# HGRN2 layers: the value projection token-major for two heads, the values matmuls moved into the next head's scores visit

## The reference, cut to what matters

```
h = rms_norm(x, norm_w[layer])
q, f, inp_v, g = jnp.split(h @ w_in, 4, axis=-1)
q = silu(q); k = (1.0 - lb) * sigmoid(-f)
log_f = log(lb + (1 - lb) * sigmoid(f))          # forget gate, per channel
# with b the running sum of log_f over the tokens, and state 0 at the start:
o[t] = sum_{s<=t} (q[t] . k[s] . exp(b[t] - b[s])) v[s]
o = rms_norm(o, o_norm_w) per head
x = x + (o * silu(g)) @ w_out
```

## Time and profile before

| | us |
|---|---|
| median of 3 runs | 1348.59 (1348.59 to 1348.66) |
| span of the profiled execution | 1346.8 |
| TensorE matmul busy in it | 1339.1 (99%) |
| VectorE busy | 923.1 (69%) |
| ScalarE busy | 687.2 (51%) |
| GpSimd busy | 145.3 (11%) |
| granted TensorE clock | 1.00 |

### The profile page before, as it was taken

How to read it: one execution, slowest core, us unless ns; L and a number is a source line. 1 busy time by engine, 2 the same in 40 slices (tenths; PEclk the granted TensorE clock), 3 DMA queues, 4 the chain that set the end, 5 groups by cost and what they waited for, 6 DMA issues and landing times.

```text
span 1346.8 us, 22178 instructions
## 1 busy us (share of the span) xinstructions
PE 1339.1 (99%) x8759; PEld 1118.0 (83%) x8759; DVE 923.1 (69%) x1659; ACT 687.2 (51%) x1226; POOL 145.3 (11%) x224
## 2 busy tenths in 40 slices
PE   9999999999999999999999999999999999999999
PEld 8888888888888888888888887788888888888887
DVE  7867778564767576666676676865657577777782
ACT  6445555353655565656565656553434335454550
POOL 2422333000000000000000000000000022332220
DMA  6322233423222222222223131332333322232221
GB/s 194 95 80 79 64 94 95 118 79 91 66 79 79 79 79 79 79 79 79 79 68 90 48 92 50 105 93 71 94 94 94 110 76 83 63 93 76 84 64 63
DMA packets 211688, 113.62 MB, mean 84 GB/s; under 512 B 3743, under 2 KB 209889, under 8 KB 211586
## 3 DMA queue, kind: packets, MB, share of 16 engines
q1 hardware_dynamic: 211202, 112.02, 28.9%
q0 software_dynamic: 384, 0.20, 0.1%
HBM read 110.10 MB, written 2.10 MB: 83 GB/s over the span
## 4 chain that ended last, share of the span: by engine, by line
PE 96%; DVE 2%; ACT 1%; issue 1%; DMA 0%; SPq 0%; ACTq 0%; DVEq 0%
PE ps L647 39%; PE ps L662 38%; PE scores L662 4%; PE ps L1088 2%; PE ps L1072 2%; PE ps L1028 2%; PE ps L881 1%; PE scores L1056 1%; PE ps L1056 1%; PE scores L852 1%; PE ps L676 1%; PE ps L883 1%; PE scores L870 1%; PE scores L819 1%; PE ps L892 1%
## 5 line engine op out<-in xcount | busy, mean ns | idle before, releaser
L647 PE MATMUL ps<-op_hi,w_hi 128*128 128x512 f32 (+1 forms) x800 | 311.7, 390 | 0.0
L647 PE MATMUL ps<-op_lo,w_hi 128*128 128x512 f32 (+1 forms) x800 | 305.4, 382 | 0.0
L647 PE MATMUL ps<-op_hi,w_lo 128*128 128x512 f32 (+1 forms) x800 | 304.5, 381 | 0.0
L662 PE MATMUL ps<-w_hi,op_hi 128*128 128x512 f32 (+1 forms) x728 | 294.0, 404 | 1.6 <-DVE op_lo L1844 1.6
L662 PE MATMUL ps<-w_lo,op_hi 128*128 128x512 f32 (+1 forms) x728 | 282.6, 388 | 0.0
L662 PE MATMUL ps<-w_hi,op_lo 128*128 128x512 f32 (+1 forms) x728 | 282.2, 388 | 0.0
L1786 DVE TENSOR_TENSOR w_lo<-raw,w_hi 128x1024 fp32r<-128x1024 f32 x200 | 245.1, 1251 | 12.4 <-ACT w_hi L1274 10.9
L1274 ACT ACTIVATE w_hi<-raw 128x1024 fp32r<-128x1024 f32 x200 | 203.0, 1052 | 26.8 <-PE ps L662 11.2
L647 PEld LDWEIGHTS ps<-op_lo,w_hi 128*128 128x128 f32 x800 | 150.4, 188 | 29.9
L647 PEld LDWEIGHTS ps<-op_hi,w_hi 128*128 128x128 f32 x800 | 150.5, 188 | 27.4 <-DVE op_lo L1829 0.2
L647 PEld LDWEIGHTS ps<-op_hi,w_lo 128*128 128x128 f32 x800 | 150.7, 188 | 27.0
(11 more groups left out here) (228 smaller groups left out, 1944.9 us busy)
## 6 DMA issues: line engine op xcount, KB each, us to landing
raw<-in_b_w_in SPq DMA_DIRECT2D x80, 512.0 KB, 3.9
raw<-in_a_w_in SPq DMA_DIRECT2D x64, 512.0 KB, 4.2
raw<-in_c_w_in SPq DMA_DIRECT2D x24, 512.0 KB, 4.1
raw<-in_a_w_out SPq DMA_DIRECT2D x16, 512.0 KB, 4.3
raw<-in_b_w_out SPq DMA_DIRECT2D x8, 512.0 KB, 4.0
raw<-in_c_w_out SPq DMA_DIRECT2D x8, 512.0 KB, 4.9
xt<-in_x SPq DMA_DIRECT2D x4, 512.0 KB, 6.2
y<-in_norm_w SPq DMA_DIRECT2D x3, 512.0 KB, 4.7
```

Source lines behind the costliest of these rows:

```text
L647: last = nc.tensor.matmul(bank, a, b, start=(k == 0 and p == 0), stop=(k == KT - 1 and p == 2))
L662: last = nc.tensor.matmul(bank, a, b, start=(k == 0 and p == 0), stop=(k == KT - 1 and p == 2))
```

## The change

The diff does four things, all in the HGRN2 layers.

1. Step range 16-23 is now `v_step`: v is projected token-major, for a pair of heads at once, two of the four token tiles in each body. An even body i does token tiles 0 and 1 of heads i and i+1, an odd one tiles 2 and 3 of the same pair. A body does 48 matmuls 256 wide in place of 24 matmuls 512 wide. The v weights of head i+1 are loaded and split in body i (body 0 has five chunks, body 7 three); four ring slots hold the v weights, `a_v01` and `a_v23` the results.
2. `turn_v`, `v_out`, `a_v`, `a_vt` and their semaphores are gone.
3. `values(h-1)` stands ahead of `scores` in the visit after step 6 of the next body, `states` and `turn_o` go from the visit after step 20 to one after step 26. The squares, the root, `o_squares` and `o_norm` of a head move into the next body with it.
4. The last move of the queries (`last_move`) writes into a buffer of its own, `a_qf`; it is two VectorE instructions (a copy of one half, a multiply of the other) in place of one. `a_on` shares the buffer of `a_sq`.

```diff
-        a_v, at = carve(at, 2, S)
+        a_v01, at = carve(at, 4, 2 * P)
+        a_v23, at = carve(at, 2, 2 * P)
-        a_vt, at = carve(at, TT, P)
-        a_on, at = carve(at, TT, P)
+        a_on = a_sq
+        a_qf, at = carve(at, S)
...
+def a_order(i):
+    of_v = ((2, 0), (2, 1)) if i == 0 else ((2, i + 1),) if i + 1 < HEADS else ()
+    return ((1, i), (0, i)) + of_v + ((3, i),)
...
+        def v_half(of):
+            return a_v23 if of % 2 else a_v01[:, of // 2 % 2 * 2:of // 2 % 2 * 2 + 2]
+        def v_tile(head, t):
+            return v_half(head // 2 * 2 + t // 2)[:, t % 2, head % 2 * P:(head % 2 + 1) * P]
...
# TensorE
-                    def turn_v():
...
+                    def v_step(k):
+                        slot = a_v_slot(i // 2 * 2)
+                        for half in (2 * k, 2 * k + 1):
+                            t, of = divmod(half, KT)
+                            last = token_step(acc[0][:, t * 2 * P:(t + 1) * 2 * P], slice(slot, slot + 2), of,
+                                              i % 2 * 2 + t)
+                        return last
...
                     def states():
-                        pe.wait_ge(vT_done, h + 1)
+                        pe.wait_ge(v_act, h // 2 * 2 + 2)
...
                     if mix and not proj:
-                        turn_v()
                         gate_bank(3, 4, 5, 6, 7)
+                        values(h - 1)
                         scores()
...
-                        steps[17] = [turn_v, turn_k]
-                        steps[20] = [turn_o, states] if end else [states]
-                        steps[25] = [values]
-                        steps[6] = [scores]
+                        steps[17] = [turn_k]
+                        steps[26] = [turn_o, states] if end else [states]
+                        steps[6] = [lambda: values(h - 1), scores] if end else [scores]
...
# ScalarE
+                    def square(of):
+                        act.wait_ge(o_ready, of + 1)
...
-                        split_chunks(IN0[n], per, j, par, (2, 3), ring)
+                        for part, of in a_order(i)[2:]:
+                            split_part(i, part, of)
...
                         nc.scalar.activation(a_sig[:, 2], acc[0][:], ACT.Sigmoid, scale=-1.0).then_inc(f_act, 1)
+                        if end:
+                            square(h - 1)
...
                         if mix:
-                            v_out()
                             k_out()
+                        if end:
+                            root(h - 1)
...
# VectorE
-                        move_queries(6, a_q2[:, 0], h, prev, 4)
+                        last_move()
...
-                    split_lo_chunk(IN0[n], len(A_PARTS), j, par, 3, ring)
+                    split_part(i, 3, i)
+                    if end:
+                        o_squares(h - 1)
...
+                    if end:
+                        o_norm(h - 1)
+                    move_queries(0, a_q[:, par], head, par, 0)
+                    far_queries(0)
+                    farthest_queries(0)
+                    if not last_proj:
+                        for part in (1, 0):
+                            split_part(i + 1, part, i + 1)
+                    next_queries(0)
+                    far_queries(1)
+                    farthest_queries(1)
                     if mix:
                         carry()
                     if end:
                         into_y()
...
-                    if mix and not last_proj:
-                        o_squares(h)
-                    next_queries(0)
-                    if mix and not last_proj:
-                        o_norm(h)
...
+                    next_queries(1)
+                    far_queries(2)
+                    farthest_queries(2)
```

More of the change, by code:

```diff
@@ L86, with a_number, a_v_slot, a_ring @@
 ACC0 = [sum(ACC_OF[:n]) for n in range(4)]
[L89 to L96, removed]
+def a_order(i):
+    of_v = ((2, 0), (2, 1)) if i == 0 else ((2, i + 1),) if i + 1 < HEADS else ()
+    return ((1, i), (0, i)) + of_v + ((3, i),)
+def a_number(i, part, head):
+    return sum(len(a_order(n)) for n in range(i)) + a_order(i).index((part, head))
+def a_v_slot(head):
+    return (HALF + 2, HALF)[head // 2 % 2] + head % 2
+def a_ring(part, head):
+    return (1, 0, a_v_slot(head), SLOTS - 1 if head == HEADS - 1 else 2)[part]
 def b_ring(par, c):
@@ L518, in load_first, with load_a @@
                 for c in chunks:
-                    w, col = ((a_w_in[n // 3], A_PARTS[c] * D) if n % 3 == 0 else
+                    w, col = ((a_w_in[n // 3], a_order(0)[c][0] * D + a_order(0)[c][1] * P) if n % 3 == 0 else
                               (b_w_in[0], B_PARTS[c] * D) if n == 1 else (c_w_in[0], D + c * P))
                     load((IN0[n] + c) % RAW, columns(w, col), IN0[n] + c)
+            def load_a(n):
+                for i in range(HEADS):
+                    for c, (part, head) in enumerate(a_order(i)):
+                        if i == 0 and c < (RAW if n else 2):
+                            continue
+                        at = IN0[n] + a_number(i, part, head)
+                        load(at % RAW, columns(a_w_in[n // 3], part * D + head * P), at)
             def load_layer(n, w, parts):
@@ L541, in _ @@
                 if t in (1, 2):
-                    load(t - 1, columns(a_w_in[0], A_PARTS[t - 1] * D), t - 1)
+                    load(t - 1, columns(a_w_in[0], a_order(0)[t - 1][0] * D), t - 1)
             for n in range(layers):
@@ L987, in body @@
                             steps[3].append(lambda k=k: wide(n, k, (2, 3)))
-                    for ks in range(len(A_PARTS) * KT):
+                    for ks in range(A_CHUNKS * KT):
                         c, k = divmod(ks, KT)
+                        part = (1, 0, 2, 3)[c]
                         if proj and static(i) and i == 0 and c < 2:
-                            last = feature_step(acc[c][:, 256:S], a_ring(par, c), k, slice(256, S))
+                            last = feature_step(acc[c][:, 256:S], a_ring(part, i), k, slice(256, S))
                             if k == KT - 1:
@@ L995, in body @@
                             if k == 0:
-                                pe.wait_ge(lo_done, chunk(IN0[n], len(A_PARTS), j, par, c) + 1)
+                                needed = (i // 2 * 2, 2, i // 2 * 2 + 1) if c == 2 else (i, part, i)
+                                pe.wait_ge(lo_done, IN0[n] + a_number(*needed) + 1)
                                 bank_free(c)
-                            last = feature_step(acc[c % 2][:], a_ring(par, c), k)
+                            last = v_step(k) if c == 2 else feature_step(acc[c % 2][:], a_ring(part, i), k)
                             if k == KT - 1:
@@ L1913, in layer_a, with split_part @@
                 H0 = HEADS * idx
+                def split_part(i, part, head):
+                    at = IN0[n] + a_number(i, part, head)
+                    split_lo(at % RAW, a_ring(part, head), at)
                 nc.vector.memset(a_ones, 1.0)
@@ L2128, in body @@
                     if proj:
-                        split_lo_chunk(IN0[n], len(A_PARTS), j, par, 2, ring)
+                        for part, of in a_order(i)[2:-1]:
+                            split_part(i, part, of)
                     if not proj:
```

105 lines of the change are left out of this document (45 added, 60 removed).

## The result

The changed kernel takes 1352.25 us (median of 8 runs, 1350.81 to 1353.49) where the kernel before takes 1348.62 us (8 runs beside it): the ratio is 1.0025, with a 95% interval of 1.0015 to 1.0036. Run again later beside the experiments it took 1350.75 us (11 runs, 1350.39 to 1353.63) against 1348.60 us: 1.0022 [1.0013, 1.0031]. It is a little slower. The forecast of 1350.0 us had the sign of the difference and 1.4 us of its 2 to 3.6 us; the time lies in the range given, 1345.0 to 1354.5 us, just past the bound of 0.2% behind which slower had 0.30 of the chance. Both intervals have that bound inside, so whether it was passed is not settled.

What follows compares the result with a forecast made beforehand. TensorE, busy 99% of the span, was taken as the bound. Its work (-2.7 us), waits at the layers' ends (+3.6) and start (+0.6) summed to +1.5 us: about 1350.0 us, range 1345.0 to 1354.5 us.

Steps and rivals of the forecast that it cites:

- the bound of 0.2%: Whole kernel: within 2.7 us of 1348.59 us counts as no change (chance 0.53); slower had 0.30, faster 0.17.
- v as 256-wide matmuls: v projection, 16 bodies: 768 matmuls at 0.1198 us replace 384 at 0.2266 us, +5.0 us (range from 0.0 us).
- Rival A: v projection: 256 columns cost half of 512, so the v step adds 0; total 1345.1 us, chance 0.13.
- `turn_v` gone, a visit fewer: TensorE in 16 bodies: transposes of v removed, 7.0 us off; 16 visits fewer, 0.7 us off; sum with v's +5.0: -2.7 us.
- Middle bodies without a new wait: Middle of a layer: `states` has 1.8 us of slack on `v_act`, so no wait; body 27.0 us where it was 27.2.
- Rival C: Visit after step 26, seven bodies a layer: `states` waits for ScalarE's copy of v, 7 to 14 us, about 1360; chance 0.20.
- The ends of the layers: End of each HGRN2 layer: VectorE's low parts 3 us later, TensorE waits 1.8 us for `y_lo(0)`, twice, +3.6 us.
- What the wait costs: Ends of both HGRN2 layers: TensorE's two waits were priced at their length alone, +3.6 us.
- The start: Body 0 of layer 0: one more split on ScalarE ahead of step 16, TensorE waits 0.6 us; nothing in layer 3.
- Rival B: Layers' ends: VectorE keeps up and `first_tile(0)` finds `y_lo(0)`, no wait; -2.1 us, 1346.5 us, chance 0.17.
- The granted clock is 1.00 throughout: Whole kernel before the change: TensorE's granted clock read as full everywhere when pricing matmul distances.

Runs made afterwards that it cites:

- x_swap: Changed kernel with the next head's scores ahead of the previous head's values in TensorE's visit, bodies 2 to 8 of both HGRN2 layers: 1350.68 us.
- x_square: Changed kernel with ScalarE squaring the previous head's values before its wait for the forget gate's bank, and VectorE summing them ahead of its masks: 1348.98 us.
- x_pool: Changed kernel with GpSimd's two last key moves of heads 7 and 15 held back until VectorE wrote y's low parts of tiles 0 and 1: 1349.18 us.
- x_again: The changed kernel itself, unaltered, run once more beside the other experiments: 1350.75 us (11 runs).
- x_busy: Changed kernel with seven unused 512-wide products filling TensorE's idle time before the output projection's first tile in both HGRN2 layers: 1351.11 us.
- x_late: Fastest version (1345.6 us) with five unused 0.6 us VectorE operations ahead of y's low parts in body 8 of both HGRN2 layers: 1351.95 us.
- x_start: Changed kernel with the gate's weights split behind the forget gate's sigmoids on ScalarE, in the first body of both HGRN2 layers: 1350.64 us.
- x_tail: Changed kernel with two output columns and the last gate's weights split in body 7 ahead of the masks, in both HGRN2 layers: 1346.49 us.
- x_values: Kernel before with only a head's values moved to the next body's visit ahead of scores, states and `turn_o` left after step 20: 1373.77 us.

## Why the prediction was right or wrong

*v as 256-wide matmuls, +5.0 us.* Right: 0.120 us a product, not 0.113. Rival A is out, and so is its 1345.1 us. By the Trainium skill, "TensorE: Matmul & The Clock Gate", section "Back-to-back issue gap", an isolated one would take 0.109 us; in this stream of weight loads and matmuls the trace shows 0.120. Why the form of the earlier trace rows takes 0.113 no run settled.

*`turn_v` gone, a visit fewer, sum -2.7 us.* Right: the traces give -3.1 us.

*Middle bodies without a new wait.* Right: 26.99 us for 27.0, no wait of the states on ScalarE. Rival C is out.

*The ends of the layers, 1.8 us each.* The size was right (1.87 and 1.54 us), two of its terms were not. The forecast let VectorE's list grow by 2.2 us for later scores and `o_squares` and by 0.8 us for `o_norm`. The scores' lateness counts only through the f bank, which TensorE fills behind the same visit: VectorE's list is tied to ScalarE's sigmoids and square, as x_swap showed, and x_square by 0.48 us. ScalarE's first sigmoid of f in the kernel before is this row:

```profile
208.66 0.60 ACT L1461 ACTIVATE scratch<-ps 128x512 f32<-128x512 f32 x1 [4.79 <-PE ps L647]
```

From f's first sigmoid to the splits of body 8 it is 228.66 - 208.97 = 19.69 us after and 227.37 - 208.66 = 18.71 us before: 1.0 us longer, of which ScalarE's square is half. With the 1.56 us by which f itself is later that is 2.5 us where the forecast had 3.0. What made up for the overestimate is a collision that the forecast does not have: two operations of VectorE's beside GpSimd's `move_keys`, 0.44 us (x_pool). The two errors cancelled, so that the sum came out at 1.8 us was in part luck. The later second tile, 0.3 us a layer, is in no term. By the Trainium skill, "SBUF — State Buffer", section "Who interferes with whom", an operation of VectorE with two inputs in SBUF contends with one of GpSimd that reads SBUF, and the later to issue waits. The trace agrees in kind: alone the pair takes 1.29 us, beside GpSimd 2.13 us, and in x_again, where VectorE's first one was issued ahead of GpSimd's, 1.71 us.

*What the wait costs.* This step failed: 3.6 us were put down for two waits, and nothing for what an idle TensorE does to its own clock. In ten of 19 executions the granted clock fell, which cost 1.6 us in the one that was profiled. x_busy took the fall away with the wait's end in its place, x_late brought it back with the idle time and nothing else of the changed ends. The medians of all executions were 1350.75 and 1352.25 us; those of the executions without a fall, 1350.7 and 1351.0 us. What decides whether an idle time of this length brings the fall stays open. Without it the forecast would still be 0.7 to 1.0 us low, about the second tile's 0.6 us.

*The start, +0.6 us.* Right: 0.44 us of wait seen, 0.8 us between the faster groups of x_start and the changed kernel. *Rival B*, no wait at the ends, had 1346.5 us; the version made so, x_tail, takes 1346.49 (1.9 us below its own runs of the kernel before, where B had 2.1).

*What the forecast read wrongly.* "The granted clock is 1.00 throughout" was read from a view without a record behind it; the kernel before, too, has its first products at half pace (eight transposes in 1.94 us). As both kernels open alike, nothing in the sum hangs on it. But the opening takes up to 1 us more in some profiles, by when it leaves that pace, and this limits how far differences below 1 us between the experiments may be read.

## What to carry to other kernels

Where an engine is 99% busy, work taken from it is worth its distance only until the next hand-over; what stands there in the other engines' lists has to be followed up to the real pacer, which is the engine that ends each wait and not the one whose input came later. Before a reorder, use idle time of the waiting engine for work that it owes later: three splits moved into idle time gained more (4 us) than the change was to bring (2.7 us). And price an idle time of TensorE at more than its length: 1.5 to 2.1 us of it cost another 1.6 us or more in part of the executions, 3.3 us of it about another 3 us (x_values).

## What the runs showed of the hardware that I had not expected

- The granted clock fell to 0.50 (1.2 GHz) after TensorE had stood idle for 2.1 us in an otherwise busy kernel, in 7 of 7 executions; with the changed kernel's 1.87 us in layer 0 (and 1.54 or 0.84 us in layer 3) in 10 of 19; in none of 33 of x_pool, x_swap and x_square, whose idle time at these places was 1.43 or 1.44 us at most. The executions are told by their mean clock, the idle times and places by one profile of each kernel. It came back within about 4 us, behind the 3.34 us of x_values within about 7 us, and the same idle time in the same execution may or may not bring it.
- Two `tensor_tensor` of 512 columns on VectorE take 2.13 us beside GpSimd's two and 1.29 us alone (x_pool), and 1.71 us when VectorE's first one was issued 0.15 us ahead of GpSimd's (x_again, layer 3).
- Small products of TensorE go at half pace at the start of the kernel, up to about 10.5 us in some profiles and 13.3 us in others, which moves the end of the opening by up to 1 us.
